# Convolution taps dealt out anew between the steps of the delta rule

## The chip, the cores and the metric

One core of one Trainium2 chip runs the whole network in one launch. The metric is the device time of that launch in microseconds, lower is better. Matrix work is done by TensorE (PE), with its weight loads (PEld); VectorE (DVE), ScalarE (ACT) and GpSimd (POOL) work beside it; SyncE (SP) issues the weights' transfers. Each engine works through its own instructions in program order and waits on semaphores for the others.

## The reference

Two residual stacks over 256 tokens of width 1024, in float32. The first has two layers of: half a gated feed-forward, a mixer, half a gated feed-forward. The change lies in this mixer. It projects the input to queries, keys, values, gates and a GLU pair, and has two branches:

```
qkv = silu(causal_dwconv(qkv, conv_w))            # 4 taps
o   = chunk_gated_delta_rule(q, k, v, g, beta)    # 8 heads of 128, chunks of 64 tokens
y_a = (rmsnorm(o) * silu(z)) @ w_o
h   = a * sigmoid(gate)                           # 1024 channels
h   = causal_dwconv(h, dw_w) + dw_b               # 31 taps
y_b = silu(layernorm(h)) @ w_o + b_o
x   = x + rmsnorm((g_a * y_a + g_b * y_b) @ mix_w_out)
```

The delta rule solves a unit lower triangular 64 x 64 system in each chunk and head, and carries a 128 x 128 state from chunk to chunk. The second stack (gated linear attention, latent attention, a short convolution, squared-ReLU feed-forwards) isn't touched.

## The kernel before

**Tiling.** The tokens are two tiles of 128, the 1024 channels eight groups of 128 partitions. Each product is made of three matmuls of split operands (high by high, high by low, low by high); ScalarE makes the high part of a weight unit (L1421), VectorE the low part (L1966), TensorE uses it at L590, where a helper records most matmuls.

**The delta rule's stage** (`mixer`) runs two generators in turn on each engine. The main one is `pairs` over `group(t, g)`: for each of two tiles t, two groups g of four heads take turns, one step each, 22 steps a group, so 44 places a tile. Places 0 to 11 are the tile's beginning (normalising, transposes, the first products, L2343 to L2374 on VectorE). Places 12 to 31 are the levels of the triangular inverse, five levels of four places: in the first two of a level VectorE masks one product for each group (L2381), the other two hold nothing of its own. Places 32 to 43 are the end: places 32 and 33 come behind the levels, places 36 and 37 and 40 and 41 follow a state update (L2398 or L2402) of the first and the second group, and places 42 and 43 lie between the output's mean (L2409), whose root GpSimd takes (L2762), and the output itself (L2416).

**The side work** (`side`) is stepped by `interleave` after the places that SIDE_AT names: four projections on TensorE, their weights' parts on ScalarE and VectorE, then the mean of the wide convolution over the channels.

**The taps.** The wide convolution runs on VectorE: `conv_taps` (L2261) is a generator that goes through channels 0 to 3, then 4 to 7, 31 taps each. Each pull from it issues the taps of two channels (L2269 for the first tap, L2273 for the others), 124 pulls a layer. `glu_` pulls 16 times and `qkv` 12 times. In the mixer `step()` (L2423) is called at each place and pulls as often as TAPS_AT (L266) says for it. The side step at place 41 of tile 1 pulls all that are left:

```
for _ in taps[0]:
    pass
dve.wait_ge(*when("ln_mean", (tag, 0)))
V.tensor_copy(lnm[:, 0:2], ps[:, 6, 0:2])
```

TensorE's side step there (`conv_mean`) waits for the last tap of each of the eight channel groups. Behind it, on VectorE, stand the output of tile 1 and what follows.

Of the kernel before, what the change touches and what calls it, by code (L numbers as in the profile page):

```python
# [17 lines left out]
NT = SEQ // P  # L18
# [22 lines left out]
LEVELS = [1, 2, 4, 8, 16, 32]  # L41
# [211 lines left out]
PAIR_STEPS = GROUPS * GROUP_STEPS  # L253
# [9 lines left out]
SIDE_AT = [0, 1, 0, 1, 0, 1, 0, 1, 0, 1, 0, 0] + [0] * _LEVELS + [1, 0, 1, 0, 1, 0, 1, 0, 0, 1, 0, 0]  # L263
SIDE_AT_END = SIDE_AT[:-12] + [1, 0, 1, 0, 0, 1, 0, 0, 0, 1, 0, 1]
SIDE_STEPS_AT = SIDE_AT * (NT - 1) + SIDE_AT_END
TAPS_AT = [0, 0, 0, 0, 2, 2, 2, 2, 0, 0, 2, 2] + [0, 1, 1, 1] * (len(LEVELS) - 1) + [2, 2, 2, 2, 1, 1, 2, 2, 1, 1, 1, 1]  # L266


def pairs(group):


    for t in range(NT):
        both = [group(t, g) for g in range(GROUPS)]
        for _ in range(GROUP_STEPS):
            for one in both:
                next(one)
                yield
        for one in both:
            for _ in one:
                assert False  # L280


def interleave(main, side):


    taken = SIDE_FIRST
    for _ in range(SIDE_FIRST):
        next(side)
    for n, _ in enumerate(main):
        if SIDE_STEPS_AT[n]:  # L290
            next(side)
            taken += 1
    assert n + 1 == MAIN_STEPS and taken == SIDE_STEPS
    for _ in side:
        assert False
# [32 lines left out]
def emit(nc, io, plan, last=None):  # L328
# [8 lines left out]
    with ctx:  # L337
# [1603 lines left out]
        def _(dve):  # L1941
# [337 lines left out]
            def side(tag):  # L2279
                for _ in range(4):  # L2280
                    for k in range(4):
                        if k:
                            weights(1)
                        yield
                    weights(1)
                    yield
# [3 lines that stand above are left out]
                V.tensor_copy(lnm[:, 0:2], ps[:, 6, 0:2]).then_inc(*up("ln_mean_out", tag))  # L2290
                yield
                dve.wait_ge(*when("ln_spread", (tag, 0)))
                V.tensor_tensor(hc[:, :, :], hc[:, :, :], over(ps[:, 7, 0:SEQ], KC),
                                ALU.subtract).then_inc(*up("ln_center", tag))
                yield
# [124 lines left out]
            def mixer(tag, i):  # L2420
                taken = [0]

                def step():  # L2423

                    for _ in range(TAPS_AT[taken[0] % PAIR_STEPS]):
                        next(taps[0], None)
                    taken[0] += 1

                interleave(pairs(lambda t, g: group(tag, t, g, step)), side(tag))
# [515 lines left out]
```

## Time and profile before

| | |
|---|---|
| median of 3 runs | 3017.79 us (3016.14 to 3019.17) |
| the profiled execution, its own time | 3015.88 us |
| its span | 3014.1 us |
| TensorE busy | 96% |
| VectorE busy | 64% |
| ScalarE busy | 51% |
| mean granted clock of TensorE | 0.977 |

The span is the time from the first to the last instruction of one profiled execution. Busy time counts instructions that compute, not those that wait. In a timeline a row gives start, duration, engine, line, operation, output and input, how often it repeats, and in brackets the idle time before it with what ended it.

### The profile page before, as it was taken

The numbers are of one execution on the slowest core, as the hardware profiler recorded it, in microseconds if no ns is written. First come the engines' busy times: TensorE is split into PE (matmuls) and PEld (weight loads), VectorE is DVE, ScalarE is ACT, GpSimd is POOL, SyncE is SP. The second block draws the span as 40 slices with busy tenths as digits, with TensorE's granted clock in tenths as the row PEclk, the third lists the DMA queues.
The fourth block names the chain that finished last, engine by engine and source line by source line (L and its number), as shares of the span: only waits on it lengthen the run. The fifth ranks groups of instructions, "written<-read, shape, count | busy, mean of one in ns | idle before, by whom it ended". The sixth has DMA issues, their size and how long they took to land.

```text
span 3014.1 us, 38314 instructions
## 1 busy us (share of the span) xinstructions
PE 2883.0 (96%) x15292; PEld 2443.9 (81%) x15292; DVE 1934.4 (64%) x2858; ACT 1537.6 (51%) x2235; POOL 73.8 (2%) x99
## 2 busy tenths in 40 slices
PE   7999998899999999988999999999999999999999
PEld 6879987678878799876788878887888878887887
DVE  5556987575565569876755676465646765567645
ACT  5544744355555447443655545555545445564554
POOL 0000000000000000000000000000000000000000
PEclk9999999899999999998999999999999999999999
DMA  7534510245555444102455525543555555453552
GB/s 280 188 134 161 175 50 22 101 168 204 189 180 189 138 161 171 54 22 92 166 210 189 177 94 208 184 175 112 200 189 181 192 185 184 158 195 109 187 183 83
DMA packets 127809, 470.03 MB, mean 156 GB/s; under 512 B 14494, under 2 KB 14654, under 8 KB 126480
## 3 DMA queue, kind: packets, MB, share of 16 engines
q1 hardware_dynamic: 124560, 453.08, 43.0%
q0 software_dynamic: 3072, 14.51, 1.4%
q8 instruction: 121, 1.98, 0.3%
q14 instruction: 56, 0.46, 0.0%
HBM read 466.48 MB, written 1.05 MB: 155 GB/s over the span
## 4 chain that ended last, share of the span: by engine, by line
PE 80%; DVE 12%; ACT 5%; issue 2%; POOL 1%; DMA 0%; SPq 0%; POOLq 0%; ACTq 0%; DVEq 0%
PE ps L590 77%; DVE w_lo_part L1966 2%; DVE hc L2273 2%; PE ps L767 2%; DVE conv_acc L2198 1%; ACT w_hi_part L1421 1%; PE ps L627 1%; DVE wx_lo_part L1966 0%; DVE h_lo_part L2009 0%; ACT wx_hi_part L1421 0%; DVE x_res L2110 0%; DVE zs L2416 0%; ACT gdn_rhs L1696 0%; POOL gdn_gate L2762 0%; DVE x_res L2168 0%
## 5 line engine op out<-in xcount | busy, mean ns | idle before, releaser
L1966 DVE TENSOR_TENSOR w_lo_part<-w_raw,w_hi_part 128x1024 fp32r<-128x1024 f32 x459 | 552.8, 1216 | 346.9 <-ACT w_hi_part L1421 344.5
L1421 ACT ACTIVATE w_hi_part<-w_raw 128x1024 fp32r<-128x1024 f32 x459 | 477.5, 1054 | 402.4 <-PE ps L590 402.1
L590 PE MATMUL ps<-w_hi_part,h_hi_part 128*128 128x512 f32 (+1 forms) x1348 | 542.3, 402 | 32.6 <-DVE w_lo_part L1963 8.3
L590 PE MATMUL ps<-w_hi_part,h_lo_part 128*128 128x512 f32 (+1 forms) x1348 | 528.6, 392 | 0.0
L590 PE MATMUL ps<-w_lo_part,h_hi_part 128*128 128x512 f32 (+1 forms) x1348 | 528.0, 392 | 0.0
L1966 DVE TENSOR_TENSOR wx_lo_part<-wx_raw,wx_hi_part 128x1024 fp32r<-128x1024 f32 x222 | 268.2, 1219 | 203.2 <-ACT wx_hi_part L1421 201.2
L1421 ACT ACTIVATE wx_hi_part<-wx_raw 128x1024 fp32r<-128x1024 f32 x222 | 231.6, 1055 | 226.5 <-PE ps L590 226.4
L590 PEld LDWEIGHTS ps<-w_hi_part,h_hi_part 128*128 128x128 f32 x1348 | 258.3, 192 | 91.5 <-issue 18.9
L590 PEld LDWEIGHTS ps<-w_hi_part,h_lo_part 128*128 128x128 f32 x1348 | 257.7, 191 | 54.7
L590 PEld LDWEIGHTS ps<-w_lo_part,h_hi_part 128*128 128x128 f32 x1348 | 258.9, 192 | 48.5
L590 PE MATMUL ps<-wx_hi_part,h_hi_part 128*128 128x512 f32 x684 | 271.4, 397 | 6.9 <-ACT lv L1759 2.2
L590 PE MATMUL ps<-wx_hi_part,h_lo_part 128*128 128x512 f32 x684 | 267.0, 390 | 0.0
L590 PE MATMUL ps<-wx_lo_part,h_hi_part 128*128 128x512 f32 x684 | 266.8, 390 | 0.0
L590 PE MATMUL ps<-w_hi_part,hid_hi_part 128*128 128x512 f32 x528 | 206.1, 390 | 0.0
L590 PE MATMUL ps<-w_hi_part,hid_lo_part 128*128 128x512 f32 x528 | 205.5, 389 | 0.0
L590 PE MATMUL ps<-w_lo_part,hid_hi_part 128*128 128x512 f32 x528 | 205.4, 389 | 0.0
L2273 DVE SCALAR_TENSOR_TENSOR hc<-glu,cols,hc 128x256 f32<-128x256 f32 x480 | 197.1, 476 | 0.0
L590 PE MATMUL ps<-h_hi_part,w_hi_part 128*128 128x256 f32 (+1 forms) x680 | 194.9, 287 | 0.0
L590 PE MATMUL ps<-h_lo_part,w_hi_part 128*128 128x256 f32 (+1 forms) x680 | 193.9, 285 | 0.0
L590 PE MATMUL ps<-h_hi_part,w_lo_part 128*128 128x256 f32 (+1 forms) x680 | 193.8, 285 | 0.0
L590 PEld LDWEIGHTS ps<-wx_hi_part,h_hi_part 128*128 128x128 f32 x684 | 128.9, 188 | 35.7 <-issue 6.9
L590 PEld LDWEIGHTS ps<-wx_hi_part,h_lo_part 128*128 128x128 f32 x684 | 128.7, 188 | 27.4
(437 smaller groups left out, 4899.1 us busy)
## 6 DMA issues: line engine op xcount, KB each, us to landing
w_raw<-in_weights SPq DMA_DIRECT2D x569, 512.0 KB, 3.3
wx_raw<-in_weights SPq DMA_DIRECT2D x288, 512.0 KB, 3.3
row<-in_rows POOLq DMA_DIRECT2D x8, 1024.0 KB, 4.9
row<-in_rows POOLq DMA_DIRECT2D x8, 512.0 KB, 4.0
const<-in_const SPq DMA_DIRECT2D x1, 1088.0 KB, 16.0
x_res<-in_x SPq DMA_DIRECT2D x2, 512.0 KB, 6.8
ple_p<-in_p POOLq DMA_DIRECT2D x4, 256.0 KB, 4.7
out<-x_res SPq DMA_DIRECT2D x2, 512.0 KB, 2.6
```

The source lines that it names most:

```text
L590: return nc.tensor.matmul(out, lhsT, rhs_, start=start, stop=stop, skip_group_check=True)
L627: last_ = nc.tensor.transpose(turned_bank(t, b)[:, c, :], src[:, t, (4 * b + c) * P:(4 * b + c + 1) * P], ident)
L767: last_ = nc.tensor.transpose(hid_bank(c, blk // 2)[:, blk % 2, t * P:(t + 1) * P], hid[:, c % 2, t, blk * P:(blk + 1) * P], ident)
L1421: A(hi_of(s)[:, 0:wd], raw_of(s)[:, 0:wd], ACT.Copy).then_inc(*up("w_hi", u))
L1966: V.tensor_tensor(lo_of(s)[:, 0:wd], raw_of(s)[:, 0:wd], hi[:, 0:wd], ALU.subtract).then_inc(*up("w_lo", u))
L2198: ins = V.scalar_tensor_tensor(cacc[:, c % 2, :], pre[:, c % 2, k:k + SEQ], col(("convw", i), c * CONV1 + k), cacc[:, c % 2, :], ALU.mult, ...
L2273: ins = V.scalar_tensor_tensor(hc[:, c, :], glu[:, c, k:k + SEQ], w, hc[:, c, :], ALU.mult, ALU.add)
```

## The change

The table of pulls is written anew, and the last tile gets an end of its own, so the table now covers both tiles instead of one that repeats:

```diff
-TAPS_AT = [0, 0, 0, 0, 2, 2, 2, 2, 0, 0, 2, 2] + [0, 1, 1, 1] * (len(LEVELS) - 1) + [2, 2, 2, 2, 1, 1, 2, 2, 1, 1, 1, 1]
+TAPS_AT = [0] * 12 + [1, 1, 1, 1] * (len(LEVELS) - 1) + [2, 2, 2, 2, 1, 1, 5, 5, 2, 1, 0, 0]
+TAPS_AT_END = TAPS_AT[:-12] + [2, 2, 3, 3, 2, 2, 4, 4, 2, 2, 0, 0]
+TAPS_AT_ALL = TAPS_AT * (NT - 1) + TAPS_AT_END
@@ mixer, VectorE
-                    for _ in range(TAPS_AT[taken[0] % PAIR_STEPS]):
+                    for _ in range(TAPS_AT_ALL[taken[0]]):
                         next(taps[0], None)
```

Everything else is as it was: the taps, their order, the places of the side steps and all other instructions.

## Rows read from the trace of the kernel before

**Rows 1.** The page: busy time of the engines, and the group of taps.
```profile
PE 2883.0 (96%) x15292; PEld 2443.9 (81%) x15292; DVE 1934.4 (64%) x2858; ACT 1537.6 (51%) x2235; POOL 73.8 (2%) x99
...
L2273 DVE SCALAR_TENSOR_TENSOR hc<-glu,cols,hc 128x256 f32<-128x256 f32 x480 | 197.1, 476 | 0.0
```

**Rows 2.** TensorE's waits by releaser: us in total, times, longest us.
```profile
PE ps L1017 <- ACT gdn_w L1704: 12.5, 4, 3.2
...
PE ps L590 <- DVE hc L2273: 8.2, 2, 4.1
...
PE ps L590 <- DVE gdn_w L2381: 5.3, 4, 1.9
```

**Rows 3.** VectorE's timeline, first layer, tile 1: the last state update and behind it.
```profile
546.47 1.12 DVE L2398 SCALAR_TENSOR_TENSOR gdn_state<-gdn_state,gdn_gate,ps 128x128 f32<-128x128 f32 x4 [2.06 <-PE ps L590]
...
549.43 11.16 DVE L2273 SCALAR_TENSOR_TENSOR hc<-glu,cols,hc 128x256 f32<-128x256 f32 x28
```

**Rows 4.** VectorE's timeline: tile 0's first two levels, and L2369 of tile 1.
```profile
402.68 3.25 DVE L2273 SCALAR_TENSOR_TENSOR hc<-glu,cols,hc 128x256 f32<-128x256 f32 x8
405.85 0.68 DVE L2381 TENSOR_TENSOR gdn_w<-ps,const 128x512 f32<-128x512 f32 x1
...
412.98 0.69 DVE L2381 TENSOR_TENSOR gdn_w<-ps,const 128x512 f32<-128x512 f32 x1 [3.48 <-PE ps L590]
413.87 0.69 DVE L2381 TENSOR_TENSOR row<-ps,const 128x512 f32<-128x512 f32 x1 [0.20 <-PE ps L590]
...
491.21 0.69 DVE L2369 TENSOR_TENSOR gdn_w<-ps,gdn_w 128x512 f32<-128x512 f32 x1 [0.40 <-PE ps L590]
```

**Rows 5.** TensorE's timeline: the same levels, and tile 1's first level.
```profile
402.70 1.06 PE L590 MATMUL ps<-gdn_w 128*128 128x128 f32 x8
...
406.58 3.65 PE L590 MATMUL ps<-gdn_w 128*128 128x128 f32 x16 [1.93 <-DVE gdn_w L2381]
410.03 1.13 PE L590 MATMUL ps<-row,xn 128*128 128x128 f32 x8
...
411.88 1.06 PE L590 MATMUL ps<-gdn_w 128*128 128x128 f32 x8
...
413.73 2.05 PE L590 MATMUL ps<-gdn_w 128*128 128x128 f32 x16
415.61 1.06 PE L590 MATMUL ps<-row,xn 128*128 128x128 f32 x8
...
503.01 2.05 PE L590 MATMUL ps<-gdn_w 128*128 128x128 f32 x16 [1.14 <-DVE gdn_w L2381]
```

**Rows 6.** Stretches: length, busy PE, PEld, DVE, ACT, POOL, granted clock, DMA share, GB/s.
```profile
404.60:411.00 6.40, 4.47 (x26) 4.42 (x26) 4.90 (x12) 1.19 (x2) 0.00 (x0) 0.73 0.13 50
...
554.00:581.00 27.00, 14.22 (x67) 12.52 (x66) 15.46 (x39) 8.05 (x14) 2.01 (x2) 0.68 0.33 128
```

**Rows 7.** GpSimd's timeline: the root of an output in tile 0 and in tile 1.
```profile
462.52 1.17 POOL L2762 TENSOR_TENSOR gdn_gate<-gdn_gate,neghalf 128x4 f32<-128x4 f32 x1 [82.24 <-DVE gdn_gate L2409]
...
565.82 1.01 POOL L2762 TENSOR_TENSOR gdn_gate<-gdn_gate,neghalf 128x4 f32<-128x4 f32 x1 [89.62 <-DVE gdn_gate L2409]
```

**Rows 8.** VectorE's timeline: the output behind each of these roots.
```profile
463.73 1.12 DVE L2416 SCALAR_TENSOR_TENSOR zs<-ps,gdn_gate,zs 128x128 f32<-128x128 f32 x4 [0.50 <-POOL gdn_gate L2762]
...
566.86 1.13 DVE L2416 SCALAR_TENSOR_TENSOR zs<-ps,gdn_gate,zs 128x128 f32<-128x128 f32 x4 [1.12 <-POOL gdn_gate L2762]
```

**Rows 9.** VectorE's and TensorE's timelines: the last level of tile 0.
```profile
429.52 0.69 DVE L2381 TENSOR_TENSOR gdn_w<-ps,const 128x512 f32<-128x512 f32 x1 [1.56 <-PE ps L590]
430.42 0.69 DVE L2381 TENSOR_TENSOR row<-ps,const 128x512 f32<-128x512 f32 x1 [0.20 <-PE ps L590]
...
431.26 1.06 PE L590 MATMUL ps<-xn,row 128*128 128x128 f32 x8
```

**Rows 10.** VectorE's timeline: the state updates of tile 0's second chunk.
```profile
454.62 1.12 DVE L2398 SCALAR_TENSOR_TENSOR gdn_state<-gdn_state,gdn_gate,ps 128x128 f32<-128x128 f32 x4 [5.04 <-PE ps L590]
...
458.60 1.12 DVE L2398 SCALAR_TENSOR_TENSOR gdn_state<-gdn_state,gdn_gate,ps 128x128 f32<-128x128 f32 x4 [2.06 <-PE ps L590]
```

## The prediction, made before the run

> **What bounds the kernel now.** I read the page first: TensorE is busy for 2883.0 of 3014.1 us, VectorE for 64%, and one tap of the wide convolution is a 476 ns instruction of which there are 480 [rows 1]. So the kernel is bound by TensorE, and a change on VectorE can move the time only through what TensorE waits for. The second view is therefore TensorE's waits by releaser [rows 2]. Three entries concern the delta rule's stage: 12.5 us in 4 waits for ScalarE (L1704, at a tile's beginning), 5.3 us in 4 waits for VectorE's L2381 (the first level of each tile), and 8.2 us in 2 waits for the taps themselves (L2273, at the end of each layer's stage). The third view is the timelines of VectorE and TensorE beside each other in that stage. There are two layers with two tiles each; the rows shown are of the first layer, and the second repeats them with its own start, 0.1 us apart or less except where I say so.
>
> **What moves.** One pull from the generator issues two taps. Back to back a tap takes 0.396 us: 28 of them take 11.16 us, and (11.16 - 0.48) / 27 = 0.396 [rows 3]. So a pull is 0.79 us. The generator gives 124 pulls a layer; 16 go in glu and 12 in qkv, 96 are left. Before, tile 0 takes 45 and tile 1 takes 12 + 15 + 16 = 43 up to the side step that drains the rest: 8 remain. After, tile 0 takes 20 + 23 = 43, tile 1 takes 20 + 26 = 46, and 7 remain. No instruction is added or removed. By place, per layer: 24 pulls leave the tile beginnings, 2 leave tile 0's output; 10 come to the levels (the first call of each level, in front of the second group's L2381), 7 to the end of tile 0 (3 + 3 + 1), and 3 to tile 1 before its last state update. 26 - 20 = 6, so 6 more pulls than before lie behind tile 1's last state update.
>
> **Gain 1: the first level of each tile.** Four pulls (places 10, 11) stand before L2381 of the first group: they run from 402.68 and L2381 starts at 405.85 [rows 4]. When could it start without them? In the next level VectorE stood idle for it, and it began at 412.98, 1.10 us behind TensorE's product at 411.88; TensorE's next product began 0.75 us behind that, at 413.73 [rows 4, 5]. So TensorE could begin at 402.70 + 1.10 + 0.75 = 404.55 instead of 406.58: 2.03 us. TensorE also ran slowly behind this wait: 16 matmuls took from 406.58 to 410.03 = 3.45 us, against 413.73 to 415.61 = 1.88 us in the next level [rows 5], and the granted clock in that stretch is 0.73 on average [rows 6], which is between the levels 1.2 and 2.4 GHz. With no wait I expect no low clock there: 1.57 us more. The other three tiles show a wait of 1.1 us with the second value of the matmuls, 2.05 us for 16 [rows 5]; with the 0.1 us by which the start moved more than the idle column says (2.03 against 1.93), they give 1.2 us each. Sum: 2.03 + 1.57 + 3 x 1.2 = 7.2 us.
>
> **The tile beginnings: nothing.** The 8 pulls of places 4 to 7 lie beside TensorE's wait for ScalarE [rows 2], whose own queue holds no tap. In tile 1 VectorE has done them and still waits 0.40 us for TensorE before L2369 [rows 4]. Only the first tile's L2369 could come earlier (0.8 us), and TensorE has a projection unit to do there. Cost and gain 0.
>
> **Gain 2: tile 0's output.** The pull between mean and output ran beside GpSimd's root. The root took 1.17 us with taps beside it and 1.01 us in tile 1, where none are [rows 7]; the output followed with 0.50 and 1.12 us of idle time [rows 8], so the tap is hidden and only the root's 0.16 us counts, twice in series. Between 0.16 and 0.33 us a layer; 0.5 us in all. The Trainium skill, page "SBUF — State Buffer", section "SBUF: two separate sides", says that a VectorE instruction with two SBUF inputs and a GpSimd instruction that reads SBUF take an exclusive lock, and that the later one fully blocks. By that the two taps would hold back each root by up to their whole length, 0.87 us, instead of 0.16, and the sum would be 4 x 0.7 = 2.8 us better; the rows of this case bear out a small delay only.
>
> **Loss 1: the levels.** A level takes 5.5 us (412.98 and the next are PE-bound, VectorE idle for 3.48 us in the first and 1.56 us in the later ones [rows 4, 9]), so one pull more fits into the time. But it stands between the two L2381. The second would start at 0.60 + 0.79 = 1.39 us behind the first, and TensorE could use it 0.75 us later, 2.14 us behind the first. TensorE wants it at 415.61, which is 2.63 us behind 412.98: 0.49 us of margin in levels 1 to 4. In the last level the first group has 8 matmuls instead of 16, and TensorE wants it at 431.26, 1.74 us behind 429.52 [rows 9]: 0.4 us late. TensorE then has no wait to give it back until the tile's end. 4 x 0.41 = 1.6 us. Bounds: 0, and 0.41 in all 20 levels = 8.2 us if the margin is not there.
>
> **Between the states of tile 0: nothing.** VectorE idled for 5.04 us before its state update at 454.62 and 2.06 us before that at 458.60 [rows 10]. 6 pulls are 4.75 us, which leaves 0.29 us; 1 pull of 0.79 fits into the second. If they overrun, nobody waits for that state before tile 1. The weights' low parts (L1966) in this stretch move by 0.4 us and belong to slots that TensorE uses several units later; TensorE shows no wait for them here.
>
> **Loss 2: behind the last state update.** That update at 546.47 waited 2.06 us for TensorE [rows 3], so it moves with TensorE. Behind it VectorE runs without a gap: 1 pull, a weight, 14 pulls; afterwards 2, a weight, 19. TensorE waits for these taps for 4.1 us in each layer [rows 2], the mean of the convolution needs them, and the output of tile 1, its transposes and gdn_out stand behind it in program order on both engines. So nothing covers them: 12 taps x 0.396 = 4.75 us, 9.5 us for two layers. Bounds: 0 if that wait were covered, 9.5 as it stands.
>
> **The sum.** -7.2 - 0.5 + 1.6 + 9.5 = +3.4 us. Layer 0 about +0.6, layer 1 about +2.8. The profiled execution took 3015.88 us and would take 3019.3; the median of the runs shown is 1.9 us higher, so I forecast 3021 us. What this kernel's measurement can tell from no change is 0.2%, 6.0 us: 3011.8 to 3023.8.
>
> **Rivals.**
> (B) Faster: the last taps are covered, so that TensorE's wait for them does not grow, and only the gains count: -7.7 + 1.6 = -6.1, 3011.7 us. For it: VectorE keeps unused idle time in tile 1. Against: the 4.1 us wait in both layers.
> (C) Slower: the added pull in front of the second L2381 holds TensorE up in every level, not in the last alone. It decides once the second product needs L2381 less than 2.14 us behind the first. 16 more times 0.41 = 6.6, so +10.0, 3027.8 us. For it: the margin is 0.49 us; against: in the rows it is the same in every level.
> (D) Slower by the clock: in the 27 us round the tap wait the granted clock is 0.68 [rows 6], and a wait of 9 us in place of 4 may leave it low for longer; or the low clock of the first tile's level comes back elsewhere. One more stretch like that of 1.57 us a layer: +3.1, 3024.3 us. TensorE is already at the lower level there, which speaks against. The Trainium skill, "TensorE: Matmul & The Clock Gate", section "What's actually happening", says that where the clock changes varies from run to run; by that rule the 1.57 us of gain 1 may be missing in some runs, and the sum then is +5.0. The trace shows one such stretch in four like places, which agrees.
> (E) Nothing changes (the drain makes up for every place): 3017.8 us. Against: the pulls before the drain differ in every stretch.
>
> **How the numbers follow.** My case 0.67, with its own range 3017 to 3025; B 0.11, C 0.09, D 0.09, E 0.04. Faster by over 0.2%: half of B and a little of mine, 0.08. Slower: C, half of D, and a sixth of my own case, 0.25. Same: 0.67. The range reaches towards B and to C: 3013 to 3027.5.
>
> **What would show it.** Right: no wait of TensorE for L2381 in the first level; a wait of 8 to 9 us in place of 4.1 for L2273 in both layers; 42 taps instead of 30 behind the last state update of tile 1; 0.4 us before the second group's last product. Wrong: TensorE waits for L2381 in the middle levels (C), the tap wait stays at about 4 us (B), or the first level's wait stays.

## The result, and the profile after

The changed kernel takes 3025.79 us (median of 8 runs, 3023.27 to 3026.84) against 3018.61 us for the kernel before (8 runs, 3016.14 to 3021.22): a ratio of 1.0022 with a 95% interval of 1.0012 to 1.0032. It is 7.2 us slower. Forecast were +3.4 us and 3021 us, so the way was right and the size half of it: 3025.79 lies in the stated range of 3013 to 3027.5, but above the 3017 to 3025 of my own case, and rival D's 3024.3 is nearer to it. At 0.22% it is also just over the 0.2% from which the prediction called a change slower (chance 0.25). Of the 4.8 us between forecast and result, 0.8 come from the base, whose median is now 3018.61 for 3017.79 us. The execution of before on which the sum was made took 3015.88 us, 2.7 us below that median; its two stages of the delta rule are not shorter for it (485.3 us in it and in e1, the same program), the difference lies outside them.

The page of the changed kernel: its first lines. TensorE is busy for 2.1 us longer than before [rows 1], so 7.5 of the 9.6 us between the two spans (3014.1 and 3023.7) are waiting. The two stages of the delta rule hold 7.4 of the 9.6 us (table below), the rest of the program 2.3.

```profile
span 3023.7 us, 38314 instructions
...
PE 2885.1 (95%) x15292; PEld 2444.8 (81%) x15292; DVE 1934.3 (64%) x2858; ACT 1537.7 (51%) x2235; POOL 73.5 (2%) x99
```

TensorE's waits in the changed kernel by releaser: us in total, times, longest us. The lines of the kernel stand two further down than before, so L2275 is the tap that was L2273, L2383 the mask that was L2381.

```profile
PE ps L592 <- DVE hc L2275: 17.7, 2, 8.9
PE ps L1019 <- ACT gdn_w L1706: 12.3, 4, 3.2
...
PE ps L592 <- DVE row L2383: 0.9, 4, 0.2
```

Against [rows 2]: the wait for the taps has grown from 4.1 to 8.9 us in each layer, the wait for ScalarE at L1019 in the tile beginnings is the same, the 5.3 us in front of the first levels are gone, and a new wait of 0.2 us for the second group's mask stands in each of the four tiles.

VectorE in the first level of tile 0, layer 0, against [rows 4]: it is there early and waits 1.86 us; the added pull stands between the two masks; and in the next level 1.06 us are left of its idle time.

```profile
406.80 0.69 DVE L2383 TENSOR_TENSOR gdn_w<-ps,const 128x512 f32<-128x512 f32 x1 [1.86 <-PE ps L592]
407.41 0.87 DVE L2275 SCALAR_TENSOR_TENSOR hc<-glu,cols,hc 128x256 f32<-128x256 f32 x2
408.20 0.68 DVE L2383 TENSOR_TENSOR row<-ps,const 128x512 f32<-128x512 f32 x1
408.80 2.46 DVE L2275 SCALAR_TENSOR_TENSOR hc<-glu,cols,hc 128x256 f32<-128x256 f32 x6
412.32 0.69 DVE L2383 TENSOR_TENSOR gdn_w<-ps,const 128x512 f32<-128x512 f32 x1 [1.06 <-PE ps L592]
```

TensorE beside it, against [rows 5] and [rows 9]: 1.84 us from the product at 405.71 to the next one at 407.55, as forecast (1.85), no wait, 16 matmuls in 1.89 us; and the new wait in the last level.

```profile
405.71 1.06 PE L592 MATMUL ps<-gdn_w 128*128 128x128 f32 x8
...
407.55 2.05 PE L592 MATMUL ps<-gdn_w 128*128 128x128 f32 x16
409.44 1.06 PE L592 MATMUL ps<-row,xn 128*128 128x128 f32 x8
...
431.00 1.16 PE L592 MATMUL ps<-xn,row 128*128 128x128 f32 x8 [0.23 <-DVE row L2383]
```

VectorE between the states of tile 0 and at its output, against [rows 10] and [rows 8]; then GpSimd's root, against [rows 7]. The six added pulls leave 0.37 us of the 5.04; the root takes 1.01 us with no tap beside it.

```profile
454.40 1.12 DVE L2400 SCALAR_TENSOR_TENSOR gdn_state<-gdn_state,gdn_gate,ps 128x128 f32<-128x128 f32 x4 [0.37 <-PE ps L592]
...
463.35 1.12 DVE L2418 SCALAR_TENSOR_TENSOR zs<-ps,gdn_gate,zs 128x128 f32<-128x128 f32 x4 [1.12 <-POOL gdn_gate L2764]
```

```profile
462.31 1.01 POOL L2764 TENSOR_TENSOR gdn_gate<-gdn_gate,neghalf 128x4 f32<-128x4 f32 x1 [81.09 <-DVE gdn_gate L2411]
```

The end of layer 0's stage: VectorE from the last state update, against [rows 3], and TensorE's wait. 4 + 38 = 42 taps where 30 were. (In tile 1 the second chunk has no state update, so the last one stands in front of place 37, and the pulls of places 37 to 41 lie behind it.)

```profile
546.74 1.12 DVE L2400 SCALAR_TENSOR_TENSOR gdn_state<-gdn_state,gdn_gate,ps 128x128 f32<-128x128 f32 x4 [1.26 <-PE ps L592]
547.78 1.67 DVE L2275 SCALAR_TENSOR_TENSOR hc<-glu,cols,hc 128x256 f32<-128x256 f32 x4
...
550.50 15.12 DVE L2275 SCALAR_TENSOR_TENSOR hc<-glu,cols,hc 128x256 f32<-128x256 f32 x38
```

```profile
554.56 1.05 PE L592 MATMUL ps<-const,hc 128*128 128x1 f32 x8
564.49 5.28 PE L592 MATMUL ps<-const,hc 128*128 128x1 f32 x24 [8.87 <-DVE hc L2275]
```

**The stage cut into stretches.** The differences of start times in TensorE's timeline, in us, for the two layers of a kernel (tile 0 and tile 1 where there are two values). "Beginning" is from a tile's first matmul to the product kk (keys by keys, 16 matmuls `ps<-gdn_w`); right before kk stands the "side unit", 12 matmuls of 512 columns of a side projection, which waits for ScalarE to empty `ga` (tile 0) or `gb` (tile 1) from PSUM. "Levels" is from kk to the right-hand sides' product, "end" from the channel mean's first matmul to the transposes of the output (L738, L740), "behind" from there to the first matmul that waits for the gated output `ga` (L2319, L2321).

```
kernel     beginning t0  levels t0     t0 to t1      beginning t1  levels t1     end           behind
before     23.27 25.22   39.33 36.91   32.75 32.73   25.14 26.66   36.91 36.90   16.79 16.79   40.58 40.59
changed    25.30 25.31   36.19 36.19   32.54 32.53   26.56 26.59   36.17 36.17   21.55 21.55   40.68 40.68
e1         25.22 25.32   37.26 36.92   32.77 32.77   25.69 25.90   36.92 36.93   16.81 16.80   40.65 40.65
e2         25.11 25.19   36.92 36.91   32.76 32.76   26.54 27.74   36.92 37.36   21.55 21.55   39.06 40.65
e3         24.99 25.29   35.67 35.70   32.77 32.77   26.50 26.75   35.67 35.69   16.80 16.81   39.06 39.04
e4         25.24 25.52   36.92 36.91   32.76 32.77   25.29 26.01   36.92 36.92   16.80 16.80   40.63 40.66
e5         25.19 25.51   35.67 35.68   32.61 32.61   24.48 24.98   35.66 35.67   10.07 10.07   40.64 40.64
e6         25.32 25.36   37.76 37.41   32.70 32.69   23.96 25.74   39.74 37.41   16.79 16.79   39.06 40.69
e7         25.07 25.43   35.68 35.67   32.59 32.61   26.71 24.92   35.70 35.67   21.54 21.55   40.69 40.49
e8         25.33 25.21   36.16 36.16   32.56 32.54   26.58 26.52   36.19 36.18   16.79 16.80   39.04 39.05
e9         25.40 25.31   36.17 36.18   32.55 32.53   26.68 26.60   36.19 36.16   21.55 21.55   40.65 40.67
e10        25.42 25.21   35.68 35.69   32.58 32.59   24.95 24.49   35.67 35.66   21.54 21.55   40.47 40.56
```

Levels without low clock, "t0 to t1" and end repeat to a few hundredths between kernels with the same placement there: they show what a placement costs. (The end is at the lower clock for most of its length in every kernel, and repeats all the same.) Three levels stretches hold low clock: before's 39.33, e6's 39.74 and e2's 37.36. Beginnings and "behind" hold stretches of low clock too, and beginnings vary by up to 3.4 us between the tiles of one execution.

### The profile page after: what moved, and what is told of

Same layout as the page of the kernel before. It is cut to its first block, busy times and chain, and to the rows that moved or that the text cites. A ratio compares the mean times of both kernels' runs of the same rounds, so it can differ in the third digit from the quotient of the medians.

```text
span 3023.7 us, 38314 instructions
## 1 busy us (share of the span) xinstructions
PE 2885.1 (95%) x15292; PEld 2444.8 (81%) x15292; DVE 1934.3 (64%) x2858; ACT 1537.7 (51%) x2235; POOL 73.5 (2%) x99
## 4 chain that ended last, share of the span: by engine, by line
PE 82%; DVE 11%; ACT 5%; issue 2%; POOL 0%; DMA 0%; POOLq 0%; ACTq 0%; DVEq 0%
PE ps L592 79%; DVE w_lo_part L1968 2%; PE ps L769 2%; DVE hc L2275 2%; DVE conv_acc L2200 1%; ACT w_hi_part L1423 1%; PE ps L629 1%; DVE wx_lo_part L1968 0%; DVE h_lo_part L2011 0%; ACT wx_hi_part L1423 0%; DVE x_res L2112 0%; ACT gdn_rhs L1698 0%; DVE x_res L2170 0%; DVE x_res L2148 0%; POOL stats L2764 0%
## 5 line engine op out<-in xcount | busy, mean ns | idle before, releaser
L2275 DVE SCALAR_TENSOR_TENSOR hc<-glu,cols,hc 128x256 f32<-128x256 f32 x480 | 197.7, 476 | 0.0
```

Of the source, the lines that this page charges most:

```text
L2275: ins = V.scalar_tensor_tensor(hc[:, c, :], glu[:, c, k:k + SEQ], w, hc[:, c, :], ALU.mult, ALU.add)
```

## The experiments

All have the computation of before; only the table of pulls differs. Each edit puts the two tables shown, and `TAPS_AT_ALL = TAPS_0 + TAPS_1`, in place of the three lines that the change added. Each was timed beside the kernel before: e1 to e4, e5 to e8, and e9 with e10 share one set of its runs.

**e1: the table of before again.**

```diff
+TAPS_0 = [0, 0, 0, 0, 2, 2, 2, 2, 0, 0, 2, 2] + [0, 1, 1, 1] * (len(LEVELS) - 1) + [2, 2, 2, 2, 1, 1, 2, 2, 1, 1, 1, 1]
+TAPS_1 = [0, 0, 0, 0, 2, 2, 2, 2, 0, 0, 2, 2] + [0, 1, 1, 1] * (len(LEVELS) - 1) + [2, 2, 2, 2, 1, 1, 2, 2, 1, 1, 1, 1]
```

> The table of before, written as two tables, so the program does the same. Both theories: 0 us against before. It is there for its trace: in the two traces so far the side unit behind TensorE's third wait of a tile's beginning took 2.85 us in layer 0 of before and 4.9 us in layer 0 of the changed kernel, at a granted clock of 1.00 and 0.55. If that is chance (theory 1), this trace shows a long unit in some other tile than before's did. If the changed table makes it (theory 2), the first product kk of tile 0 in layer 0 comes 23.3 us behind the stage's first matmul here too.

Measured: 3020.10 us against 3018.99 (ratio 1.0003, 0.9994 to 1.0012). In this trace the first product kk of layer 0 comes 25.2 us behind the stage's start, not 23.3, and the first level's wait is followed by matmuls at full pace. The side unit in the beginning, in before's trace and in this one (stretch, its length, busy times, granted clock, DMA share, GB/s):

```profile
389.98:392.83 2.85, 2.85 (x12) 2.35 (x13) 2.85 (x7) 1.89 (x4) 0.00 (x0) 1.00 0.11 29
1221.77:1226.57 4.80, 4.80 (x12) 3.79 (x13) 4.80 (x11) 1.89 (x4) 0.00 (x0) 0.56 0.33 117
```

```profile
393.50:398.29 4.79, 4.79 (x13) 3.80 (x14) 4.79 (x11) 1.89 (x4) 0.00 (x0) 0.56 0.36 126
```

```profile
411.60 2.05 PE L592 MATMUL ps<-gdn_w 128*128 128x128 f32 x16 [1.49 <-DVE gdn_w L2383]
```

```profile
389.98 0.50 PE L590 MATMUL ps<-w_hi_part,h_hi_part 128*128 128x512 f32 x1 [0.47 <-ACT ga L1649]
```

```profile
393.50 0.80 PE L592 MATMUL ps<-w_hi_part,h_hi_part 128*128 128x512 f32 x1 [1.04 <-ACT ga L1651]
```

The five fences are the units of before, the unit of e1 in layer 0, the first matmuls of e1 behind the wait for the first level, and the first matmul of the unit in layer 0 of before and of e1. So the same program has both patterns: either the unit is slow and the level isn't, or the unit is fast, TensorE comes to the level earlier, waits there for longer (1.93 us for 1.1) and runs slowly behind that wait. In before's layer 0 these sum to 2.85 + 39.33 = 42.18 us, in its layer 1 to 4.80 + 36.91 = 41.71. e6 shows the same exchange in tile 1: 23.96 + 39.74 = 63.70 us for beginning and levels in layer 0, 25.74 + 37.41 = 63.15 in layer 1. Of the 2.42 us by which before's slow level was longer, 1.95 were thus the other side of a fast unit. It isn't a law: in e4's tile 1 of layer 0 the unit took 2.83 us and the level 36.92, and where the level's wait is gone, in e5 and e10, a fast unit is followed by a fast level.

**e2: six pulls a layer left to the end.**

```diff
+TAPS_0 = [0, 0, 0, 0, 2, 1, 1, 1, 0, 0, 2, 2] + [0, 1, 1, 1] * (len(LEVELS) - 1) + [2, 2, 2, 2, 1, 1, 2, 2, 1, 1, 1, 1]
+TAPS_1 = [0, 0, 0, 0, 2, 1, 1, 1, 0, 0, 2, 2] + [0, 1, 1, 1] * (len(LEVELS) - 1) + [2, 2, 2, 2, 1, 1, 2, 2, 1, 1, 1, 1]
```

> Before's table with 3 pulls a tile taken from the tile beginnings and nothing put elsewhere, so that 21 pulls in place of 15 stand behind the last state update of a layer. Theory 1 (the taps at the end are covered by nothing): 12 taps x 0.396 = 4.75 us a layer, +9.5 us; TensorE's wait for L2273 grows from 4.1 to 8.9 us. Rival (part of the tail is covered or the clock pays for it): +5 us or less.

Measured: 3027.55 us, +8.6 (ratio 1.0027, 1.0016 to 1.0037). The end grows from 16.8 to 21.55 us in both layers, 4.75 us each, and TensorE's waits say the same:

```profile
PE ps L592 <- DVE hc L2275: 17.8, 2, 8.9
```

The tail's price stands, 9.5 us in the two ends; the median shows 0.9 less, inside its interval.

**e3: the first levels freed.**

```diff
+TAPS_0 = [0, 0, 0, 0, 2, 2, 2, 2, 0, 0, 0, 0] + [0, 1, 1, 1] * (len(LEVELS) - 1) + [2, 2, 2, 2, 1, 1, 4, 4, 1, 1, 1, 1]
+TAPS_1 = [0, 0, 0, 0, 2, 2, 2, 2, 0, 0, 0, 0] + [0, 1, 1, 1] * (len(LEVELS) - 1) + [2, 2, 2, 5, 2, 1, 2, 2, 1, 1, 1, 1]
```

> Before's table with the 4 pulls in front of each tile's first level moved to places where VectorE stood idle (between the states), 15 pulls behind the last state update as before. Theory 1: the waits for L2381 go, 2.03 + 3 x 1.2 = 5.6 us, less what the low clock costs elsewhere: -5.6 if the low clock of layer 0's first level only moves to the tile's beginning, -7.2 if it is gone. Rival: 0, because TensorE waits for something else there.

Measured: 3010.84 us, -8.2 (ratio 0.9976, 0.9966 to 0.9987). The levels take 35.7 us in place of 36.9 in all four tiles: 4 x 1.23 = 4.9 us, my 1.2 a tile. The median gives more than either number of the expectation (5.6 or 7.2), though its interval (4 to 10 us) holds both. The rest was not expected in this place: "behind" is 39.05 us in place of 40.65 in both layers (3.2 us), while tile 1's beginnings are 0.8 us longer each than in e1. VectorE is ready for the first mask 1.48 us before TensorE:

```profile
408.45 0.69 DVE L2383 TENSOR_TENSOR gdn_w<-ps,const 128x512 f32<-128x512 f32 x1 [1.48 <-PE ps L592]
```

**e4: the tile beginnings emptied.**

```diff
+TAPS_0 = [0, 0, 0, 0, 0, 0, 0, 0, 0, 0, 2, 2] + [0, 2, 1, 1] * (len(LEVELS) - 1) + [2, 2, 2, 2, 1, 1, 3, 4, 1, 1, 1, 1]
+TAPS_1 = [0, 0, 0, 0, 0, 0, 0, 0, 0, 0, 2, 2] + [0, 2, 1, 1] * (len(LEVELS) - 1) + [2, 2, 2, 5, 1, 1, 2, 2, 1, 1, 1, 1]
```

> Before's table with the 8 pulls of places 4 to 7 moved to levels and states, behind the second group's L2381 (not in front of it), the rest as before, 15 pulls behind the last state update. Theory 1: 0 us, the tile beginnings wait for ScalarE whatever VectorE does. Theory 2 (empty beginnings lengthen the stretch of low clock at the side unit): +3.5 us, the product kk of each tile 1.5 to 2 us later as in the changed kernel.

Measured: 3019.20 us against 3018.99 (ratio 1.0000, 0.9991 to 1.0009). Emptying costs and gains nothing: VectorE then idles in front of L2371 (once L2369), and TensorE comes no sooner. Theory 2, that empty beginnings by themselves lengthen the low clock there, falls: the four beginnings sum to 102.1 us here and in e1.

```profile
399.46 0.69 DVE L2371 TENSOR_TENSOR gdn_w<-ps,gdn_w 128x512 f32<-128x512 f32 x1 [5.68 <-PE ps L592]
```

**e6: a pull between the two masks.** Before's table but for the levels, `[1, 1, 1, 0]`:

```diff
+TAPS_0 = [0, 0, 0, 0, 2, 2, 2, 2, 0, 0, 2, 2] + [1, 1, 1, 0] * (len(LEVELS) - 1) + [2, 2, 2, 2, 1, 1, 2, 2, 1, 1, 1, 1]
+TAPS_1 = [0, 0, 0, 0, 2, 2, 2, 2, 0, 0, 2, 2] + [1, 1, 1, 0] * (len(LEVELS) - 1) + [2, 2, 2, 2, 1, 1, 2, 2, 1, 1, 1, 1]
```

> Before's table with one pull of each level in front of the second group's L2381 in place of the level's last one. Theory 1 (only the last level has no margin): 4 x 0.4 = +1.6 us, a wait of 0.2 us for L2381 in each tile's last level. Rival C (each level holds TensorE up): +8 us.

Measured: 3018.93 us against 3018.93 (ratio 1.0001, 0.9992 to 1.0009). The trace has the mechanism: 0.5 us in each level stretch without low clock (37.41 for 36.91), the wait in the last level alone,

```profile
PE ps L592 <- DVE row L2383: 0.9, 4, 0.2
```

and C's price in every level is not there. The time doesn't show the 2 us, though its interval (-2.4 to +2.7 us) holds them; in this execution one "behind" of 39.06 us gives back 1.6. Whether the pull costs 2 us in all is inconclusive by time, what it does to the levels is clear by trace, and C's +8 us is excluded by both.

**e8: the changed table with the old tail.**

```diff
+TAPS_0 = [0, 0, 0, 0, 2, 1, 0, 0, 0, 0, 0, 0] + [1, 1, 1, 1] * (len(LEVELS) - 1) + [2, 2, 2, 2, 1, 1, 5, 5, 2, 1, 0, 0]
+TAPS_1 = [0, 0, 0, 0, 2, 1, 0, 0, 0, 0, 0, 0] + [1, 1, 1, 1] * (len(LEVELS) - 1) + [2, 2, 3, 3, 2, 2, 4, 4, 2, 2, 0, 0]
```

> The changed table with 6 of its pulls a layer (3 a tile) put back at places 4 and 5 of the tile beginnings, so that 15 pulls stand behind the last state update, as before the change. Theory 1: the tail's cost goes, -8.6 to -9.5 us against the changed kernel: 3016 to 3017 us, 2 to 3 us faster than before. If the whole table's loss is not the tail's, it stays above before.

Measured: 3009.90 us, 9.0 faster than before (ratio 0.9969, 0.9957 to 0.9982), so without the longer tail the change is a gain. I expected 2 to 3 us faster than before, and 8.6 to 9.5 faster than the changed kernel; its median is 15.9 below that one's. Its trace beside the changed kernel's: ends 16.8 for 21.55 us (9.5 in all) and "behind" 39.05 for 40.68 (3.3), every other stretch alike to 0.1 us. TensorE's wait for the taps is that of before again:

```profile
PE ps L592 <- DVE hc L2275: 8.2, 2, 4.1
```

**e7 and e10: the added pull behind the second mask.** The changed table with `[0, 2, 1, 1]` in the levels; run twice, the second time beside the changed kernel (e9).

```diff
+TAPS_0 = [0, 0, 0, 0, 0, 0, 0, 0, 0, 0, 0, 0] + [0, 2, 1, 1] * (len(LEVELS) - 1) + [2, 2, 2, 2, 1, 1, 5, 5, 2, 1, 0, 0]
+TAPS_1 = [0, 0, 0, 0, 0, 0, 0, 0, 0, 0, 0, 0] + [0, 2, 1, 1] * (len(LEVELS) - 1) + [2, 2, 3, 3, 2, 2, 4, 4, 2, 2, 0, 0]
```

> The changed table with its added pull of each level behind the second group's L2381. Theory 1: -1.6 us against the changed kernel, so +5 to +6 us against before. If the placement in the level costs more than that, it comes nearer to before.

> The changed kernel once more, beside e10 on one chip, for a second trace and for a comparison that isn't across chips. Theory 1: +7 us against before. The stretches that hold no low clock (kk to the rhs products 36.2 us, the end of TensorE's own work to the output's transposes 21.55 us) are as in its first trace; those that hold one (the side unit 2.8 to 5.2 us, the stretch behind the transposes 39.05 or 40.65 us) may differ.

> The kernel of e7 once more. Theory 1: four times 0.5 us, so 2 us faster than e9. Rival (the place in the level is worth 6.7 us, as e7 and the first run of the changed kernel, on different chips, seemed to say): 6 to 7 us faster than e9.

Measured: e7 3019.12 us (before 3018.93; ratio 1.0004, 0.9995 to 1.0012), 6.7 below the changed kernel's first median where 1.6 were expected; e9 3024.90 us (before 3018.61; ratio 1.0020, 1.0012 to 1.0029); e10 3017.48 us (ratio 0.9993, 0.9983 to 1.0003). So e10 is 7.4 us faster than e9 where I expected 2, and the rival's number came out, for the second time: moving this one pull of each level takes the whole loss of the change away, though 42 taps still stand at the end. The levels give 0.5 us a tile, 2.0 in all, as expected. The traces put the larger part elsewhere: in tile 1's beginnings, 26.7 and 26.6 us in e9 and 24.95 and 24.5 in e10, 3.8 us together. TensorE in layer 1 of e9, the tile's first matmuls and kk (26.60 us apart), then of e10 (24.49 us apart):

```profile
1299.61 2.08 PE L592 MATMUL ps<-const,gdn_gate 128*128 128x128 f32 x8 [3.21 <-DVE zs L2418]
...
1321.08 0.80 PE L592 MATMUL ps<-w_hi_part,h_hi_part 128*128 128x512 f32 x1 [1.61 <-ACT gb L1651]
1326.21 1.95 PE L592 MATMUL ps<-gdn_w 128*128 128x128 f32 x16
```

```profile
1298.08 2.07 PE L592 MATMUL ps<-const,gdn_gate 128*128 128x128 f32 x8 [3.21 <-DVE zs L2418]
...
1319.70 0.50 PE L592 MATMUL ps<-w_hi_part,h_hi_part 128*128 128x512 f32 x1 [1.69 <-ACT gb L1651]
1322.57 1.95 PE L592 MATMUL ps<-gdn_w 128*128 128x128 f32 x16
```

Nearly the same waits, but the unit behind them takes 5.13 us at a granted clock of 0.52 in one and 2.87 at 1.00 in the other. e10's single executions lie between 3008.89 and 3023.36 us, so this isn't the same in each of them.

**e5: pulls only where VectorE was idle.** The version that the others point to.

```diff
+TAPS_0 = [0, 0, 0, 0, 2, 2, 2, 2, 0, 0, 0, 0] + [0, 2, 1, 1] * (len(LEVELS) - 1) + [2, 2, 2, 2, 1, 1, 5, 5, 2, 1, 0, 0]
+TAPS_1 = [0, 0, 0, 0, 2, 2, 2, 2, 0, 0, 0, 0] + [0, 2, 1, 1] * (len(LEVELS) - 1) + [2, 2, 4, 5, 3, 1, 0, 0, 0, 0, 0, 0]
```

> Pulls only where VectorE waited for TensorE or ScalarE: places 4 to 7 (8 a tile), four in each level, all behind the second group's L2381, 6 more between the states of tile 0, 7 more in tile 1 before its last state update. 1 pull in place of 15 is left behind that update. Theory 1: the waits for L2381 go (4.9 us), the waits for the taps go (8.2 us), and the channel mean's 24 matmuls run without a wait before them, 5.3 down to about 2.7 us each layer (5.2 us): -18 us, about 3001 us. Rival (the clock or another chain behind the taps takes it back): the wait for the taps moves to the output and less than half, -9 us, is left.

Measured: 2997.09 us against 3018.93 (ratio 0.9927, 0.9914 to 0.9939), 21.8 us faster than before and 28.7 than the changed kernel's median. About 3001 us was expected, so this is 4 us better. The ends are 10.07 us in place of 16.8, 13.4 us in all, as the expectation had it (8.2 + 5.2): the mean's 32 matmuls run in one piece. The levels give the expected 4.9; tile 1's beginnings are 2.1 us shorter than in e1, which was not expected.

```profile
554.21 3.73 PE L592 MATMUL ps<-const,hc 128*128 128x1 f32 x32
558.19 1.22 PE L592 MATMUL ps<-const,conv_ln 128*128 128x128 f32 x4 [0.25 <-DVE conv_ln L2292]
```

## Why the prediction was right, and where its size was off

The way was right for the reason given: the tail costs more than the freed levels save. The size was off by 3.9 us of the stages' time, nearly all of it low clock in the tile beginnings.

**The tail (+9.5): right.** 4.75 us a layer were forecast, the end stretch grew by 4.76 (16.79 to 21.55), in the changed kernel, e2, e7, e9 and e10 alike; e8 takes it away and the kernel is faster than before.

**The first levels (-7.2) beside the beginnings (0): 4.9 of it right, and the rest is the step that failed.** The prediction said: "With no wait I expect no low clock there: 1.57 us more." The wait and the low clock behind it did go; no levels stretch of a kernel without that wait holds any. But this term, and the 0.8 us by which that tile's wait was longer than the others' (2.03 for 1.2), were taken from one tile of one execution, in which the low clock had fallen on the level and spared the side unit before it, while the beginnings were put at nothing. e1, the same program, has the slow unit and the full pace in that level. The changed kernel has the slow unit in all four tiles, 4.88 to 5.12 us at a granted clock of 0.52 to 0.55. Its four side units:

```profile
390.92:395.80 4.88, 4.88 (x12) 3.84 (x13) 0.30 (x1) 1.89 (x4) 0.00 (x0) 0.55 0.35 121
485.99:491.09 5.10, 5.10 (x12) 4.00 (x13) 0.29 (x1) 1.90 (x4) 0.00 (x0) 0.52 0.03 10
1227.16:1232.05 4.89, 4.89 (x13) 3.84 (x14) 0.30 (x1) 1.90 (x4) 0.00 (x0) 0.55 0.33 108
1322.24:1327.36 5.12, 5.12 (x13) 4.01 (x14) 0.30 (x1) 1.90 (x4) 0.00 (x0) 0.52 0.01 4
```

Measured for the placement alone: 4 x 1.23 = 4.9 us (e3's levels), and more low clock in the beginnings: 103.8 us for the four of the changed kernel, 102.1 in e1, +1.6. Against the execution on which the sum was made, the levels did shrink by 7.3 us (39.33 + 3 x 36.91 down to 4 x 35.68, by e3 and e7), but its four beginnings sum to 100.3, and they took 3.5 back.

**The pull in the levels (+1.6): right in the levels, 2.0 measured.** 0.50 us a tile (36.18 against 35.68 in e7), in the last level alone; the margin of 0.49 us in the other levels held, so C did not happen as told. What the placement is worth in the time is not settled: 6.7 and 7.4 us in the changed table (e7, e10), 0.0 in before's (e6).

**The output of tile 0 (-0.5): right.** "t0 to t1" went from 32.76 to 32.54 us, 0.2 a layer, and the root from 1.17 to 1.01. By the exclusive lock that the Trainium skill describes (page "SBUF — State Buffer", section "SBUF: two separate sides"), 2.8 us more would have gone; that is the prediction's estimate. The traces don't agree: before's four roots with two taps beside them took 1.17 us each, its four without took 1.01, and the two taps their usual 0.87.

**The tile beginnings and the states of tile 0 (0): right as placements,** by e4 (3019.2 against 3019.0 us) and by the 0.37 us left over. The low clock in the beginnings is the failed step above.

**The sum with the measured terms:** -4.9 - 0.4 + 2.0 + 9.5 = +6.2 us for the placements, +1.6 for the low clock in the beginnings is 7.8 against e1, whose first level in turn holds 0.3 us more; the two stages of the changed kernel are in fact 7.3 us longer than e1's, and the medians differ by 7.2. So close an agreement is partly luck, since the rest of the program also differs by up to 2.7 us between these executions. Rival D was thus partly true, in its second form: low clock like that of the first tile's level came back at another place. Its first form stays open: behind the longer tap wait the stretch took 40.68 us, hardly more than before's 40.58, but e8, with the same table and the short wait, took 39.05 in both layers, while e2 had 39.06 once behind the long wait.

**Open.** Why "behind" takes 39.05 us in e3 and e8 and 40.65 in most others, and why tile 1's beginning is slow in all four cases of the changed kernel (and in e2, e3 and e8) and in only one of four in e7 and e10. What sets the clock there was not varied by itself. How much hangs on it shows when the placements alone are summed as above and set beside the measured difference from before, in us:

```
kernel       placements   measured
changed      +6.2         +7.2 (e9: +6.3)
e1            0.0         +1.1
e2           +9.5         +8.6
e3           -4.9         -8.2
e4            0.0         +0.2
e5          -18.6        -21.8
e6           +1.8          0.0
e7, e10      +4.2         +0.2, -1.1
e8           -3.3         -9.0
```

The placements order the kernels, except where their sums lie within 4.2 us of each other. Up to 6 us of a single difference isn't theirs, so neither e8's 15.9 us nor e10's 7.4 is the price of its edit alone.

## What to carry to other kernels

When work on a second engine is spread by hand, count what is left behind the last point where the bound engine still has work: there it costs its full length (here 0.79 us a pull), while pulls in the second engine's idle time cost nothing, as long as none stands in front of something that the bound engine is about to need. Emptying a place where the bound engine waits for a third engine buys nothing. A low clock seen once in one tile is no term of a sum until another tile or a second execution of the same program shows it too.

## What the runs showed of the hardware

The stretches of low clock are a property of an execution as much as of a program: a unit of 12 matmuls with 512 columns took 2.85 us at a granted clock of 1.00 in one execution and 4.79 at 0.56 in another of the same program (before, e1), and behind nearly equal waits of 3.0 and 1.6 to 1.7 us it took 5.13 at 0.52 in e9 and 2.87 at 1.00 in e10. Where it was fast the next level could be slow. Among tables that move VectorE's work without changing TensorE's order, a stretch far behind the edit took 39.05 or 40.65 us, so differences of a few us between two placements were not additive here: e8 and the changed kernel differ by 13.4 us of span for a tail of 9.5. GpSimd's root took 1.17 us with two taps of VectorE beside it and 1.01 without.
